# State-space scan, router and first expert task put together as one piece

## What is computed

```
def ssd_mixer(h, ...):                     # h = rmsnorm_2(x, ssd_norm_w), rmsnorm_2(x, w) = x * rsqrt(mean(x^2) + eps) * w
    zxbcdt = h @ w_in                      # z 2048 | xbc 4096 | dt 32 columns
    xbc = silu(causal_conv4(xbc) + conv_b)
    dt = softplus(dt + dt_bias); a = -exp(a_log)
    y = ssd_scan(xs, dt, a, bm, cm) + d_skip * xs      # 8 groups of 4 heads, state 128, chunks of 128 tokens
    y = rmsnorm_2(y * silu(z), gate_norm_w, SSM_NORM_EPS)
    return y @ w_out

def moe_swiglu(h, w_router, w_gate, w_up, w_down):     # h = rmsnorm_2(x, moe_norm_w), 8 experts, hidden width 3584
    logits = t @ w_router
    top_val, top_idx = top_k(logits, 2); gates = softmax(top_val)
    out = sum over e of combine[:, e] * (silu(t @ w_gate[e]) * (t @ w_up[e])) @ w_down[e]
x = x + ssd_mixer(...); x = x + moe_swiglu(...); return rmsnorm_2(x, final_norm_w)
```

## Time and profile before

| | value |
|---|---|
| median of 3 runs | 2021.45 us (2019.12 to 2024.08) |
| profiled execution, its own time | 2020.94 us |
| its span | 2019.0 us |
| PE busy | 1906.8 us, 94% |
| DVE busy / ACT busy / POOL busy | 1503.7 / 1247.1 / 256.6 us |
| HBM read | 493.31 MB, 245 GB/s over the span |

### The profile page before, as it was taken

One profiled execution on the slowest core, in us unless ns is written; L12 is line 12 of the kernel. 1 busy time (PEld: TensorE's weight loads), 2 busy tenths in 40 slices (PEclk: granted clock), 3 DMA queues, 4 the chain that ended last, 5 costly groups with the idle time before them and its releaser, 6 DMA issues.

```text
span 2019.0 us, 28762 instructions
## 1 busy us (share of the span) xinstructions
PE 1906.8 (94%) x10194; PEld 1635.6 (81%) x10194; DVE 1503.7 (74%) x1796; ACT 1247.1 (62%) x1603; POOL 256.6 (13%) x249
## 2 busy tenths in 40 slices
PE   8999999988999998969599999999999999999997
PEld 6888799978998997757588788887888878888785
DVE  6686665565444686453498998989989899898996
ACT  5646454434444565553377777777777777777775
POOL 2130020000000000230100400404004040040400
PEclk9999999998999898989699999999999999999998
DMA  8434555543555454300599998999999999999993
GB/s 306 139 105 138 195 178 171 198 152 105 188 168 167 139 195 139 113 1 11 197 364 355 331 378 322 362 353 330 381 331 361 343 333 379 329 358 350 339 375 133
DMA packets 215391, 495.23 MB, mean 245 GB/s; under 512 B 10452, under 2 KB 16914, under 8 KB 215330
## 3 DMA queue, kind: packets, MB, share of 16 engines
q1 hardware_dynamic: 215042, 493.34, 68.8%
q0 software_dynamic: 288, 1.05, 0.1%
HBM read 493.31 MB, written 1.05 MB: 245 GB/s over the span
## 4 chain that ended last, share of the span: by engine, by line
PE 85%; DVE 7%; ACT 4%; issue 3%; DMA 1%; DVEq 0%; SPq 0%; ACTq 0%
PE ps L249 26%; PE ps L251 25%; PE ps L250 25%; DVE w_lo L243 3%; PE ps L2214 2%; ACT w_hi L235 1%; PE ps L2233 1%; DVE a_lo L1669 1%; ACT a_hi L1117 1%; PE ps L1874 1%; PE ps L2164 0%; PE ps L2143 0%; ACT arena L1078 0%; PE ps L2276 0%; PE ps L357 0%
## 5 line engine op out<-in xcount | busy, mean ns | idle before, releaser
L243 DVE TENSOR_TENSOR w_lo<-raw,w_hi 128x1024 fp32r<-128x1024 f32 x940 | 1121.2, 1243 | 256.4 <-ACT w_hi L235 255.9
L235 ACT ACTIVATE w_hi<-raw 128x1024 fp32r<-128x1024 f32 x940 | 942.5, 1056 | 394.8 <-PE ps L251 391.9
L249 PE MATMUL ps<-w_hi,a_hi 128*128 128x512 f32 (+3 forms) x1952 | 774.0, 397 | 15.7 <-DVE w_lo L243 7.2
L251 PE MATMUL ps<-w_hi,a_lo 128*128 128x512 f32 (+3 forms) x1952 | 763.2, 391 | 0.0
L250 PE MATMUL ps<-w_lo,a_hi 128*128 128x512 f32 (+3 forms) x1952 | 762.6, 391 | 0.0
L249 PEld LDWEIGHTS ps<-w_hi,a_hi 128*128 128x128 f32 x1952 | 369.6, 189 | 100.8 <-DVE w_lo L243 15.7
L251 PEld LDWEIGHTS ps<-w_hi,a_lo 128*128 128x128 f32 x1952 | 369.4, 189 | 81.1
L250 PEld LDWEIGHTS ps<-w_lo,a_hi 128*128 128x128 f32 x1952 | 370.1, 190 | 75.6
L249 PE MATMUL ps<-a_hi,w_hi 128*128 128x256 f32 x960 | 273.7, 285 | 3.4 <-issue 2.9
L250 PE MATMUL ps<-a_lo,w_hi 128*128 128x256 f32 x960 | 273.2, 285 | 0.0
L251 PE MATMUL ps<-a_hi,w_lo 128*128 128x256 f32 x960 | 273.1, 284 | 0.0
(11 more groups left out here) (302 smaller groups left out, 1253.7 us busy)
## 6 DMA issues: line engine op xcount, KB each, us to landing
raw<-in_moe_w_gate_dram SPq DMA_DIRECT2D x112, 1024.0 KB, 7.0
raw<-in_moe_w_up_dram SPq DMA_DIRECT2D x112, 1024.0 KB, 7.0
raw<-in_moe_w_down_dram SPq DMA_DIRECT2D x112, 1024.0 KB, 6.6
raw<-in_ssd_w_in_dram SPq DMA_DIRECT2D x24, 1024.0 KB, 5.2
raw<-in_w_in_dram SPq DMA_DIRECT2D x22, 1024.0 KB, 7.0
raw<-in_w_ffn_in_dram SPq DMA_DIRECT2D x20, 1024.0 KB, 5.2
raw<-in_w_ffn_out_dram SPq DMA_DIRECT2D x11, 1024.0 KB, 5.0
raw<-in_dense_w_down_dram SPq DMA_DIRECT2D x11, 1024.0 KB, 4.9
```

The costliest lines, as they stand in the source:

```text
L235: nc.scalar.activation(w_hi[:, u % SPL, part], raw[:, u % RAW, part], ACT.Copy).then_inc(hi_done, 1)
L243: last = nc.vector.tensor_tensor(w_lo[:, u % SPL, part], raw[:, u % RAW, part], w_hi[:, u % SPL, part].bitcast(F32), ALU.subtract)
L249: nc.tensor.matmul(o, lh, rh, start=start, stop=False, skip_group_check=True)
L251: return nc.tensor.matmul(o, ll, rh, start=False, stop=stop, skip_group_check=True)
```

## The change

dt is computed with the weights as the stationary side, giving 32 rows of 256 tokens (24 matmuls), copied to SBUF by DVE, and turned back by two small transposes in the middle of the first xbc block. The split of X0 + 2 moves ahead of the softplus. The cumulative sums are taken before convolution blocks 6 and 7. The first z block is computed before the transposes of cv. The first two `tile_weights` come before the last z block; the decays of these tiles come before its SiLU. In the scan `s_ex` has three buffers, PE issues weights k + 2 ahead of output k, the state matmul is a step of its own, and DVE gates each tile with z as soon as it is summed. The norm over y is no longer applied to y: y is turned without it (in two halves, the second within the projection), ACT takes the squares during the projection, and DVE multiplies the projected result by 1/rms where it is added to x.

In the router x is transposed without the norm, the norm's weight is multiplied into the router's weights, and 1/rms into the logits. The expert tokens `h` get the norm's weight in `norm_dve` from a broadcast copy that POOL loads. Expert 0 always gets at least one task and so is always the first: its weights are loaded without the table, M0 and M0 + 1 are split during the output projection, M0 + 2 during the router. The pick is made before the diagonals; the slots by row follow the first gate projection. Tokens are split in two pieces of 512 columns instead of eight of 128, in every task.

```
@@ norm_dve
+                if name == "moe":
+                    dve.wait_ge(s_moe_g, 16)
+                    nc.vector.scalar_tensor_tensor(h[:, t, :], x[:, t, :], rstd[:, t:t + 1], moe_g, ALU.mult,
+                                                   ALU.mult).then_inc(h_ready, 1)
...
-        s_ex, s_cb = (region(13312, HPG, P), region(13824, HPG, P)), region(14336, P)
+        s_ex = (region(13312, HPG, P), region(13824, HPG, P), gla[:, 0, 0])
+        s_cb = region(14336, P)
...
@@ sync: the expert loads
-                sp.wait_ge(r_tab, 1)
-                n_tasks = sp.value_load(tasks[0:1, 15:16], min_val=1, max_val=MAX_TASKS)
...
-                with sp.Fori(0, n_tasks) as i:
...
+                task_loads(slice(0, 1), 0)
+                sp.wait_ge(r_tab, 1)
+                n_tasks = sp.value_load(tasks[0:1, 15:16], min_val=2, max_val=MAX_TASKS)
+                with sp.Fori(1, n_tasks) as i:
...
@@ scalar
+                for b in range(3):
+                    split_hi(act, Z0 + 2 * b + 3)
+                    split_hi(act, Z0 + 2 * b + 4)
+                    z_out(b)
+                decays(0)
+                decays(1)
+                split_hi(act, O0 + 1)
+                z_out(3)
...
+                    if k + 2 < 2 * NG:
+                        decays(k + 2)
+                    if k == 4:
+                        split_hi(act, O0 + 2)
+                turn_gain_act(act, "y", chunks_two(a0_hi, a1_hi), DC, lambda c: V_GN + c)
+                split_hi(act, O0 + 3)
+                split_hi(act, O0 + 4)
+                turn_gain_act(act, "y", chunks_two(a0_hi, a1_hi), 2 * DC, lambda c: V_GN + c, DC)
+                split_hi(act, O0 + 5)
+                sqrt_table(act)
                 for t in range(T):
                     C.link(nc.scalar.activation(ssd_junk, xs[:, t, :], ACT.Square, accum_out=ss[:, t:t + 1]))
                 nc.scalar.activation(sd, ss, ACT.Sqrt, scale=1.0 / DI, bias=SSM_EPS).then_inc(sq_sum, T)
...
+                for u in range(6, 10):
                     split_hi(act, O0 + u)
...
+                        act.wait_ge(m_gather, 2 * i + b + 1)
+                        nc.scalar.activation(a0_hi[:, 4 * b:4 * b + 4, 0:P], ps[6 + b][:, :].rearrange("p (c s) -> p c s", c=4),
+                                             ACT.Copy).then_inc(m_ahi, 1)
...
@@ vector: accumulate(k)
                     last.then_inc(st_acc, 1)
+                    dve.wait_ge(st_acc, k + 1)
+                    zv = zs[:, t, g * 256:(g + 1) * 256].rearrange("p (r e) -> p r e", r=HPG)
+                    nc.vector.tensor_tensor(xv, xv, zv, ALU.mult).then_inc(st_gate, 1)
...
-                nc.vector.tensor_tensor(xs, xs, zs, ALU.mult).then_inc(sy_gated, 1)
...
+                nc.vector.tensor_tensor(wr[:, :, :], wr[:, :, :], bcast(vec[:, V_MOE:V_MOE + DC], 2, NE), ALU.mult).then_inc(r_w, 1)
                 dve.wait_ge(sq_sum, 12)
...
+                        nc.vector.scalar_tensor_tensor(x[:, t, at], ps[4 + 2 * t + half][:, :], rstd[:, t:t + 1], x[:, t, at],
+                                                       ALU.mult, ALU.add).then_inc(x_new, 1)
...
+                C.link(nc.vector.tensor_tensor(nb, nb, first_e, ALU.max))
...
@@ tensor
                 tile_weights(0)
                 tile_weights(1)
+                pe.wait_ge(zs_done, 2)
+                mm_rows(pe, Z0 + 6, ps[6:8])
+                pe.wait_ge(zs_done, 3)
                 for k in range(2 * NG):
-                    tile_output(k)
+                    if k and k % 2 == 0:
+                        tile_state(k // 2)
                     if k + 2 < 2 * NG:
                         tile_weights(k + 2)
...
+                    tile_output(k)
+                    if k == 0:
+                        pe.wait_ge(zs_done, 4)
+                        tile_state(0)
+                    if k == 2 * NG - 2:
+                        pe.wait_ge(st_gate, 8)
+                        turn_gain_pe(pe, "y", xs, 2 * DC, (0,), (0, 1))
...
+                project(0, ps[2], 0, 0)
+                slots_by_row()
                 project(2, ps[3], 0)
+                pe.wait_ge(r_g, 1)
```

More of the change, by code:

```diff
@@ L359, in turn_norm_pe, with turn_gain_pe @@
                         last.then_inc(done, 1)
-        def turn_gain_pe(pe, name, src, chunks):
-            for q in range(chunks // 8):
-                for b in range(4):
+        def turn_gain_pe(pe, name, src, chunks, parts=None, banks=range(4)):
+            for q in parts or range(chunks // 8):
+                for b in banks:
                     if q:
@@ L378, in turn_act, with turn_gain_act @@
                                      ACT.Copy).then_inc(turn_hi, 2)
-        def turn_gain_act(act, name, dst_hi, chunks, gain):
-            for c in range(chunks):
+        def turn_gain_act(act, name, dst_hi, chunks, gain, first=0):
+            for c in range(first, chunks):
                 if c % 8 < 4:
@@ L395, in turn_dve, with turn_gain_dve @@
                                         dst_hi(2 * b, 2).bitcast(F32), ALU.subtract).then_inc(turn_lo, 2)
-        def turn_gain_dve(dve, name, dst_hi, dst_lo, chunks, gain):
-            for c in range(chunks):
+        def turn_gain_dve(dve, name, dst_hi, dst_lo, chunks, gain, first=0):
+            for c in range(first, chunks):
                 dve.wait_ge(turn_hi, 2 * TURN[name] + c + 1)
@@ L1535, in _ @@
                 nc.vector.tensor_tensor(tend, ps[7][:, 64:128], acs, ALU.subtract).then_inc(sd_te, 1)
+                for b in range(6, 8):
+                    conv_block(b, 0, b)
                 for r in range(1, 10, 2):
@@ new lines, in _ @@
+                weights(0)
+                weights(1)
+                split_lo(dve, O0 + 1)
+                dve.wait_ge(zs_done, 4)
+                for k in range(2 * NG):
+                    accumulate(k)
+                    if k + 2 < 2 * NG:
+                        weights(k + 2)
+                    if k == 4:
+                        split_lo(dve, O0 + 2)
+                turn_gain_dve(dve, "y", chunks_two(a0_hi, a1_hi), chunks_two(a0_lo, a1_lo), DC, lambda c: V_GN + c)
+                split_lo(dve, O0 + 3)
@@ L1574, in _ @@
+                split_lo(dve, O0 + 4)
+                turn_gain_dve(dve, "y", chunks_two(a0_hi, a1_hi), chunks_two(a0_lo, a1_lo), 2 * DC, lambda c: V_GN + c, DC)
+                for u in range(5, 10):
+                    split_lo(dve, O0 + u)
+                nc.vector.tensor_tensor(wr[:, :, :], wr[:, :, :], bcast(vec[:, V_MOE:V_MOE + DC], 2, NE), ALU.mult).then_inc(r_w, 1)
                 dve.wait_ge(sq_sum, 12)
-                C.link(nc.vector.reciprocal(rstd, sd))
+                nc.vector.reciprocal(rstd, sd).then_inc(sy_rstd, 1)
@@ L1576, in _ @@
+                dve.wait_ge(sy_rstd, 1)
                 for t in range(T):
[L1577 to L1582 removed]
+                    if t == 0:
+                        dve.wait_ge(tile_done, 6)
+                    else:
+                        dve.wait_ge(unit_used, used(O0 + 7))
+                    for half in range(2):
+                        at = slice(half * 512, (half + 1) * 512)
+                        nc.vector.scalar_tensor_tensor(x[:, t, at], ps[4 + 2 * t + half][:, :], rstd[:, t:t + 1], x[:, t, at],
+                                                       ALU.mult, ALU.add).then_inc(x_new, 1)
@@ L1642, in _ @@
                     C.link(nc.vector.tensor_reduce(pos[c], pr, AX.X, ALU.add))
+                for t in range(T):
+                    last = nc.vector.tensor_scalar(m_pt[:, t, :], iota_row, pos[0][:, t:t + 1], None, ALU.is_equal)
+                C.link(last)
+                for t in range(T):
+                    last = nc.vector.scalar_tensor_tensor(m_p[:, t, :], iota_row, pos[1][:, t:t + 1], m_pt[:, t, :],
+                                                          ALU.is_equal, ALU.add)
+                last.then_inc(m_pk, 1)
                 for n, v in enumerate(pos + gate):
@@ L2216, in gather, with project @@
                                                     start=(t == 0), stop=(t == T - 1))
-                    last.then_inc(m_gather, 1)
-                def project(u, bank, rounds):
+                        if c % 4 == 3:
+                            last.then_inc(m_gather, 1)
+                def project(u, bank, rounds, tokens=None):
                     for half in range(2):
+                        if tokens is not None:
+                            pe.wait_ge(m_alo, 2 * tokens + half + 1)
                         pe.wait_ge(lo_done, RAW * rounds + (M0 + u + half + 1))
```

274 lines of the change are left out of this document (138 added, 136 removed).

## The result

The changed kernel takes 1945.21 us, the median of 4 runs (1943.95 to 1947.65), against 2021.74 for the kernel before on the same chip (4 runs, 2019.12 to 2024.08): the ratio is 0.9623, with a 95% interval of 0.9607 to 0.9640. The profiled execution has a span of 1942.2 us against 2019.0: 76.8 us less, where the prediction summed 60.5.

What follows compares the result with a forecast made beforehand. PE was taken to bound the expert stage, but not the other stretches touched, read as chains between heavy PE streams. Six terms summed to -60.5 on 2020.94 us, 1960.4; forecast 1961, range 1948 to 1987.

Steps and rivals of the forecast that it cites:

- 1. dt projection: State-space dt projection: 48 matmuls of 32 columns become 24 of 256, -2.7 us, bounds -5 and -1.
- 2. Last convolution to the fourth scan tile: Before the scan: first z block fills PE's SiLU wait, tile 3 starts earlier, -15.3 us, bounds -11 and -17.
- 3. Tiles 3 to 15: Scan loop: a pair of tiles falls from 5.61 to 5.2 us, -2.3 in all, bounds -5 and +6.
- The rival in which VectorE and GpSimd bound the scan: Scan: DVE's queue and POOL set the pace, a pair costs 6.4 us, total 1975; chance 0.20.
- 4. Tile 15 to the projection: Scan end to output projection: norm's factor applied at x's update, squares beside the projection, -16.0 us, bounds -17.5 and -12.
- 5. Router: Router: x transposed directly, pick made first, fewer pieces behind the gather, net -19.2 us, bounds -23 and -13.
- the clock stays up in the router: Router rival: PE's gap shrinks to pieces, logits take 3.8 us and slots_by_row 1.9, total 1955; chance 0.13.
- 6. Expert tasks: Expert stage: shorter PE waits for w_lo through two token pieces, -5 us, bounds -7 and 0.
- take 0.8 off DVE and about as much off ACT: Expert tasks: two token pieces of 0.69 us replace eight per engine; gain taken as 7 x 0.8 less a rest.
- ninth task: Expert stage rival: an empty expert 0, forced first, adds a whole task of 126 us, total 2087; chance 0.02.
- opposite clocks: Range's low end: all better bounds sum to -74.5; 1.5 us allowed because they need opposite clocks, giving 1948.
- the 1.4 us that the prediction left out: ScalarE around the scan: the skill page's 1.38 us drain per table switch; prediction took the trace row and added nothing.

Runs made afterwards that it cites:

- the added wait: Kernel after, with the router's transposes of x also waiting for ScalarE's squares' sum of the MoE norm: 1949.24 us.
- the last kernel: Kernel after with the O0+2 split moved out of the scan and constant matmuls filling PE's gaps, re-sized in the router: 1935.92 us, ratio 0.9573 to the kernel before.
- the first filled kernel: Kernel after with unread matmuls of constants added before four norm waits and in the router's two gaps: 1942.72 us.

## Why the prediction was off

The measured numbers of the six terms are distances between the landmarks shown above, in the two profiled executions.

**1. dt projection: mis-sized, -2.7 said, -7.0 measured up to the last convolution matmul.** (On the traces' axes it is -7.9, but 0.9 of it is there already when the norm's transposes start, at 668.5 and 667.6, ahead of anything that was changed: that much is the difference of two executions.) The step that failed is "the clock dip that follows the norm stays and now meets main matmuls". The norm's dip does stay (it ends at 673), but there was a second one, 675 to 685, which belonged to the narrow matmuls. It held the convolution's matmuls at half speed over some 5 us beyond dt. The trace of the kernel before had it: the prediction read the second half of dt at the low clock, but gave it to the norm's dip, though the clock was at 1.00 in between. Shown by the dt projection alone, 6.9 us.

**2. Last convolution to the fourth scan tile: right, -15.3 said, -15.0 measured.** Its largest part, the z block in front of the transposes, is shown by an experiment (9 us). Within it two errors cancel, which is luck: the transposes took 4.5 instead of 6.1 us, as no dip stood before them, and from the end of z to tile 3 it was 10.3 us where 8.7 was said.

**3. Tiles 3 to 15: -2.3 said, -0.6 measured.** Pairs came at 4.9 instead of 5.2, which gained; the split at k = 4, priced at 1.5, cost 4.6 to 4.8, which lost more. The sum left out that the split also slows GpSimd and lets the clock fall. And the third buffer, named as a cause, is none for the steady pair. The rival in which VectorE and GpSimd bound the scan is false for the steady pair, and true for this one tile.

**4. Tile 15 to the projection: right.** 3.7 us said and 3.7 measured. The projection grew from 44.5 to 46.3 us by the turned second half, 1.7 where 2.4 was taken. -16.7 against -16.0. No experiment undid this step; it rests on the two traces.

**5. Router: mis-sized, -19.2 said, -23.2 measured.** The failed step is "Seven us of logits stay at the low clock": they took 3.71. That is 3.3 of the 4.0 us; with the added wait they took 6.97 again. Another 1.3 is `slots_by_row`, which took 1.7 at full clock where 3 was set. The 3.2 behind the gather came as summed, but by its second reason: the piece sizes make 0.7 of it, and the first half standing beside the gather's second half the rest. This is the rival "the clock stays up in the router", in part: the rank matmuls and most of the gather were still at 1.2 GHz, at 0.60 a pair and 5.72 us against 0.39 and 3.73 in the last kernel. That the clock stayed up through the logits was close: in three other kernels it fell earlier behind the projection's end. The pick's delay is borne out one to one, for the part of it that was tried.

**6. Expert tasks: mis-sized, -5 said, -13.4 measured.** The step "take 0.8 off DVE and about as much off ACT" had both savings, and the sum counted one: 7 x 0.8. They add, 1.57 x 7 = 11.0. Another 1.7 us came from a dip behind the start of the first project in the kernel before, at 999.5 to 1002.9, which the sum didn't have, and the rest came at the end, mostly from the clock in the last scatter matmuls. The better bound of -7 was taken from the idle view's 7.2 us, and that view leaves out that the matmuls around each wait stand further apart. The DMA, at 0.98 and 354 GB/s, did not refuse it.

Together the terms err by 4.3, 0.3, 1.7, 0.7, 4.0 and 8.4 us, the second and third in the other direction; with the 0.9 us ahead of the first term this is the 16.3 between -60.5 and -76.8. No ninth task came. The range failed because term 1 passed its better bound by 2 us and term 6 its by 6.4, the one with an unseen dip, the other with an idle time as its floor. The 1.5 us given up for "opposite clocks" are the smaller part.

## What to carry to other kernels

Price a stall by start-to-start distances around it and by the clock behind it, not by the idle time alone: here 1.0 us of idle time was 1.57, and the same 32 small matmuls cost 3.7 or 7.0 us by the clock that they met. Take a period from one point of a task to the same point of the next, not from a first and a last row. When two engines hand work to each other in one chain, add both savings. Keep wide VectorE work with two SBUF inputs away from a stretch in which GpSimd feeds TensorE, and once the big waits are gone, work without a purpose in the short ones can still pay, if it is sized below the gap at either clock: three filling matmuls at 1.2 GHz took 5.5 us in a gap of 3.3 and delayed what followed.

## What the runs showed of the hardware

The clock doesn't follow the last gap alone. Behind the same transposes, with the same waits of 0.63 and 0.22 us, PE fell to 1.2 GHz 7.0 us after the output projection's end in the kernel after, 4.6 us after it in the kernel with the z block behind, and 4.2 us after it in the first filled kernel; with the added waits it was 3.5 us. The logits take 3.7, 5.3, 5.7 and 7.0 us by that. What decides it isn't settled by these runs.

Matmuls of 512 columns that follow each other start 0.2267 us apart in the first half of the output projection and 0.2341 in the second, in both kernels, at full clock (kernel after: switch at 888 us). What changes there is the tile with the stationary operand, from a0 to a1. No run tests whether its place is the reason; it makes 0.7 us of 23.

The table loads of ScalarE around the scan took 1.28 us each in the kernel after too (at 808.69, 814.40 and 821.62 us). Behind the first and the last the next instruction started 0.01 to 0.02 us after the load's end, as in the earlier trace rows; behind the second ScalarE waited for PE. So no drain beside the load, the 1.4 us that the prediction left out, shows here.
